# Eight chunks of a modulation product as VectorE dots inside the projections of a later stage

## The reference

```
silu_c = silu(c); silu_cc = silu(c_ctx)
mod_x = silu_c  @ ada_w[layer] + ada_b[layer]
mod_c = silu_cc @ ada_w[layer] + ada_b[layer]
sh1, sc1, g1, sh2, sc2, g2 = split(mod_x, 6)      # the same for mod_c
hx = modulate(rmsnorm(x, norm1_g), sh1, sc1)
x  = x + g1 * (mixer(hx, hc) @ w_out)
x  = x + g2 * squared_relu_mlp(modulate(rmsnorm(x, norm2_g), sh2, sc2))
```

## Time and profile before

| | |
|---|---|
| median of the 3 runs shown | 1949.41 us (1945.05 to 1955.72) |
| span of the profiled execution, first to last instruction | 1942.8 us |
| the profiled execution's own time | not among the times shown; the median lies 6.6 us above the span |
| TensorE busy | 1860.4 us (96%) |
| VectorE, ScalarE, GpSimd busy | 820.1, 585.6, 381.8 us |
| read from HBM | 427.11 MB, mean 220 GB/s |
| mean granted TensorE clock | 0.989 |

### The profile page before, as it was taken

One profiled execution on the slowest core, in us unless ns is written; L12 is line 12 of the kernel. 1 busy time (PEld: TensorE's weight loads), 2 busy tenths in 40 slices (PEclk: granted clock), 3 DMA queues, 4 the chain that ended last, 5 costly groups with the idle time before them and its releaser, 6 DMA issues.

```text
span 1942.8 us, 26199 instructions
## 1 busy us (share of the span) xinstructions
PE 1860.4 (96%) x11266; PEld 1357.8 (70%) x11266; DVE 820.1 (42%) x1345; ACT 585.6 (30%) x892; POOL 381.8 (20%) x201
## 2 busy tenths in 40 slices
PE   6999999999999999999999899999999999889998
PEld 2777796964444344347887757888888788679998
DVE  2625255731111111116342844556665625674333
ACT  2523103231111111113112535222333511544554
POOL 2000000110000000006002031433334150025664
PEclk9999999999999999999999999999999999999999
DMA  9569917679999999992224004345444232414550
GB/s 357 184 239 362 328 44 283 228 305 428 427 427 427 428 427 428 427 401 86 87 87 146 20 33 166 137 174 184 163 152 151 101 117 88 176 51 167 184 196 33
DMA packets 111426, 429.84 MB, mean 221 GB/s; under 512 B 5707, under 2 KB 8822, under 8 KB 98513
## 3 DMA queue, kind: packets, MB, share of 16 engines
q1 hardware_dynamic: 109056, 416.56, 55.3%
q0 software_dynamic: 2256, 11.62, 1.6%
HBM read 427.11 MB, written 1.05 MB: 220 GB/s over the span
## 4 chain that ended last, share of the span: by engine, by line
PE 65%; DMA 17%; DVE 5%; PEld 5%; ACT 3%; issue 3%; POOL 1%; PEldq 0%; SPq 0%; ACTq 0%; POOLq 0%; DVEq 0%
PE bank L572 64%; DMA ring<-in_moe_w_down 7%; PEld bank L572 5%; DMA H<-in_moe_w_down 4%; DMA arena<-in_moe_w_down 4%; DMA X<-in_ctx 1%; PE bank L587 1%; DMA ring<-in_w_in 0%; DVE arena L2541 0%; PEldq L551 0%; DVE ring_low L2617 0%; DVE H L2011 0%; POOL H L1873 0%; DVE ring_low L2193 0%; DVE ring_low L2611 0%
## 5 line engine op out<-in xcount | busy, mean ns | idle before, releaser
L572 PE MATMUL bank<-arena_r,ring_low 128*128 128x512 f32 (+2 forms) x1920 | 594.0, 341 | 1.6 <-DVE H_low L2018 1.0
L572 PE MATMUL bank<-arena_r 128*128 128x256 f32 (+1 forms) x2176 | 589.6, 339 | 5.4 <-POOL arena_r L1966 1.8
L572 PEld LDWEIGHTS bank<-arena_r 128*128 128x128 f32 x2176 | 383.0, 189 | 57.8 <-issue 9.8
L572 PE MATMUL bank<-arena 128*128 128x64 bf16 (+8 forms) x2892 | 362.8, 318 | 41.4 <-DMA arena<-in_hy_filt_w 11.5
L572 PEld LDWEIGHTS bank<-arena_r,ring_low 128*128 128x128 f32 (+1 forms) x1920 | 350.7, 187 | 47.4 <-issue 2.6
L572 PEld LDWEIGHTS bank<-arena 128*128 128x128 bf16 (+4 forms) x2892 | 203.9, 131 | 201.5 <-issue 171.6
L572 PE MATMUL bank<-H_low,arena_r 128*128 128x512 f32 (+1 forms) x672 | 216.3, 339 | 0.0
L572 PE MATMUL bank<-ring,arena 128*64 128x512 f32 x768 | 170.4, 599 | 7.6 <-DMA ring<-in_moe_w_down 7.6
L2599 DVE SCALAR_TENSOR_TENSOR X<-bank,mod,X 128x256 f32<-128x256 f32 x216 | 94.2, 479 | 195.1 <-PE bank L572 195.1
L1950 POOL TENSOR_TENSOR ring_low<-ring,arena_r 128x2048 fp32r<-128x2048 f32 x31 | 142.3, 4613 | 130.0 <-DVE ring_low L2611 68.8
L1426 ACT ACTIVATE arena<-bank 128x512 f32<-128x512 f32 (+2 forms) x106 | 51.1, 496 | 358.5 <-PE bank L572 358.5
(11 more groups left out here) (328 smaller groups left out, 1845.4 us busy)
## 6 DMA issues: line engine op xcount, KB each, us to landing
ring<-in_w_mlp SPq DMA_DIRECT2D x32, 2048.0 KB, 7.8
ring<-in_w_in SPq DMA_DIRECT2D x26, 2048.0 KB, 8.6
ring<-in_ada_w SPq DMA_DIRECT2D x24, 2048.0 KB, 12.2
ring<-in_moe_w_up SPq DMA_DIRECT2D x17, 2048.0 KB, 23.3
ring<-in_moe_w_gate SPq DMA_DIRECT2D x17, 2048.0 KB, 27.8
arena<-in_moe_w_up SPq DMA_DIRECT2D x15, 2048.0 KB, 22.4
ring<-in_moe_w_down SPq DMA_DIRECT2D x14, 2048.0 KB, 23.3
arena<-in_moe_w_down SPq DMA_DIRECT2D x13, 2048.0 KB, 23.7
```

The lines of the kernel that those rows point to most:

```text
L572: ins = nc.tensor.matmul(o, l, r, start=start, stop=stop, skip_group_check=True)
```

## The change

- Modulation chunks 4 to 11 of the second block's first layer are no longer loaded by SP nor multiplied by TensorE. Four chunks stay, all in "hyena" (`GATE_ADA` has four places, the group has four). "projected" has none behind w_in 5, 6 and 7, and `ada_turn(5, ...)`, its copy and its `take_chunk` in "scan_b" go.
- Their 32 blocks of 128 outputs are made on VectorE in l0_in: `block_dots`, two dots of 1024 per block, from `ada_t`, a transposed copy that the host makes. GpSimd brings the blocks, the first 16 in pairs (1 MB) into two places lent by GV and YT, the rest singly (512 KB) into the two halves of the second place; each waits until the place is free. Before it writes GV (j = 5) ScalarE waits for 16 blocks, before YT's second half (j = 6) for all 32.
- In l0_in ScalarE makes the high half of chunks 1 to 6 (`chunk_high`), after the second tile of the chunk before; VectorE only subtracts (`chunk_low`).
- `CSIL` gets a place of its own and is brought and put through Silu early (in "projected" and in expert pair 2) instead of in layer 0's MLP. GpSimd's space for descriptors is set to 8192.

```diff
@@ TensorE and SP, "projected" to "hyena"
-        BEHIND = [[], [0, 1], [2, 3], [4, 5], [6, 7], [8, 9], [10, 11], [12, 13, 14]]
+        BEHIND = [[], [0, 1], [2, 3], [4, 5], [6, 7], [], [], []]
...
-            return WIN + j + sum(len(b) for b in BEHIND[:j]) if j < 8 else WIN + (23, 24, 27, 30)[j - 8]
-
-        GATE_ADA = [WIN + 25, WIN + 26, WIN + 28, WIN + 29, WIN + 31]
+            return WIN + j + sum(len(b) for b in BEHIND[:j]) if j < 8 else WIN + (16, 17, 19, 22)[j - 8]
+
+        GATE_ADA = [WIN + 18, WIN + 20, WIN + 21, WIN + 23]
...
                 load(n, cols(T["w_in"], WIN_ORDER[j] * 512, 512), as_cols(n))
-                for i in BEHIND[j] if j < 8 else ([], [15, 16], [17, 18], [19])[j - 8]:
...
-                    ada_turn(5, 7, 1, 7)
-                    pe.wait_ge(S("ada_out"), 2 + 6)
...
-            ada(GATE_ADA[0], 6, 6, 0, 5)
+            ada(GATE_ADA[0], 5, 6, 0, 4)
...
-            ada(GATE_ADA[1], 6, 6, 1, 5)
             for nt in range(2):
                 gate_tile(10, nt)
...
@@ places
-        ROT = A3(23968, 4, L)
+        ROT, DOT = A3(23968, 4, L), A(23968, D)
...
+        BLOCKS, LENT = 32, 16
+        BLOCK_PAIRS = [A3(o, 2, D) for o in (6144, 10240)]
+
+        def block_slot(q):
+
+            return BLOCK_PAIRS[(q // 2) % 2 if q < LENT else 1][:, q % 2, :]
...
@@ ScalarE
+                if p == 2:
+                    for s in range(2):
+                        act.wait_ge(S(f"blocks_in{s}"), 16)
+                    A_(CSIL, CSIL, ACT.Silu).then_inc(S("silu_c"), 1)
...
+                def chunk_high(j):
+
+                    n = first + 2 * j
+                    act.wait_ge(full[n % RING], arrived(n))
+                    act.wait_ge(used, n + 1 - RING + 1)
+                    A_(low(n + 1), slot(n), ACT.Copy).then_inc(S("high_copied"), 1)
+
+                if l == 0:
+                    chunk_high(1)
                 for j in range(8):
                     for nt in range(1 if j == 7 else 4):
                         o = tile()
+                        if l == 0 and nt == 0 and j in (5, 6):
+                            act.wait_ge(S("dots"), (LENT, BLOCKS)[j - 5])
...
+                        if l == 0 and nt == 1 and 1 <= j < 6:
+                            chunk_high(j + 1)
...
@@ GpSimd
+            def bring_pair(i):
+
+                if i >= 2:
+                    pool.wait_ge(S("dots"), 2 * (i - 1))
+                bring(BLOCK_PAIRS[i % 2], T["ada_t"][2 * i * P:2 * (i + 1) * P, :].rearrange("(b p) d -> p b d", p=P), f"blocks_in{i % 2}")
+
+            def bring_block(q):
+
+                pool.wait_ge(S("dots"), max(LENT, q - 1))
+                bring(block_slot(q), T["ada_t"][q * P:(q + 1) * P, :], f"blocks_in{q % 2}")
...
+                    pool.wait_ge(S("silu_c"), 2)
+                    for i in range(2):
+                        bring_pair(i)
...
                 for h in range(1, 2 + 2 * l):
                     head_args(h)
+                if l == 0:
+                    for i in range(2, LENT // 2):
+                        bring_pair(i)
+                    for q in range(LENT, BLOCKS):
+                        bring_block(q)
...
-                if l == 0:
-                    bring(CSIL, T["c_all_2"].rearrange("p (a d) -> p a d", a=2), "b2_in")
...
@@ VectorE
+                def block_dots(a, n):
+
+                    dve.wait_ge(S("silu_c"), 2)
+                    for q in range(a, a + n):
+                        dve.wait_ge(S(f"blocks_in{(q // 2 if q < LENT else q) % 2}"), block_arrived(q))
+                        for c in range(2):
+                            d = V.scalar_tensor_tensor(DOT, block_slot(q), 1.0, CSIL[:, c, :], ALU.mult, ALU.mult,
+                                                       accum_out=mod[:, 1, 16 + q, c:c + 1])
+                            if c == 0:
+                                link(d)
+                        d.then_inc(S("dots"), 1)
+                        dve.wait_ge(S("dots"), q + 1)
+
+                def chunk_low(j):
+
+                    n = first + 2 * j
+                    dve.wait_ge(S("high_copied"), 10 + j)
+                    V.tensor_tensor(low(n), slot(n), low(n + 1).bitcast(F32), ALU.subtract).then_inc(full[(n + 1) % RING], 16)
+
                 for j in range(1 + l, 5):
-                    split_chunk(first + 2 * j)
+                    if l:
+                        split_chunk(first + 2 * j)
+                        continue
+                    chunk_low(j)
+                    block_dots((0, 5, 11, 17)[j - 1], (5, 6, 6, 5)[j - 1])
...
                 for j in range(5, 7):
-                    split_chunk(first + 2 * j)
+                    if l:
+                        split_chunk(first + 2 * j)
+                        continue
+                    chunk_low(j)
+                    block_dots((22, 28)[j - 5], (6, 4)[j - 5])
...
@@ host
-    nc = _bacc.Bacc("TRN2", target_bir_lowering=False, num_devices=1)
+    nc = _bacc.Bacc("TRN2", target_bir_lowering=False, num_devices=1, dynamic_dma_scratch_size=8192)
```

More of the change, by code:

```diff
@@ L177, in build @@
         et = sb("chunk_decay", [P, 64])
+        CSIL = sb("silu_rows", [P, 2 * D])[:, :].rearrange("p (a d) -> p a d", a=2)
         AR = 25600
@@ L307, in _ @@
                 load(n, cols(T["w_in"], WIN_ORDER[j] * 512, 512), as_cols(n))
-                for i in BEHIND[j] if j < 8 else ([], [15, 16], [17, 18], [19])[j - 8]:
+                for i in BEHIND[j] if j < 8 else ([], [8], [9, 10], [11])[j - 8]:
                     n += 1
@@ L525, in build, with block_arrived @@
         MLP_BANK = (4, 5, 2, 3)
-        CSIL, CPROD = A3(12288, 2, D), A3(22944, 2, D)
+        CPROD = A3(22944, 2, D)
+        BLOCKS, LENT = 32, 16
+        BLOCK_PAIRS = [A3(o, 2, D) for o in (6144, 10240)]
+        def block_slot(q):
+            return BLOCK_PAIRS[(q // 2) % 2 if q < LENT else 1][:, q % 2, :]
+        def block_arrived(q):
+            return 32 + 16 * (q // 4) if q < LENT else 32 + 16 * (LENT // 4 + (q - LENT) // 2)
         W1h_cols, W2h_rows = W1h.rearrange("p (k n) -> p k n", k=KT), W2h.rearrange("p (k n) -> p k n", k=4)
@@ L848, in _ @@
             chunk_used()
-            ada(GATE_ADA[2], 6, 6, 2, 5)
+            ada(GATE_ADA[1], 5, 6, 1, 4)
             pe.wait_ge(S("un_ready"), 2)
             spectrum_half(0)
-            ada(GATE_ADA[3], 6, 6, 3, 5)
+            ada(GATE_ADA[2], 5, 6, 2, 4)
             for nt in range(2):
@@ L858, in _ @@
             chunk_used()
-            ada(GATE_ADA[4], 6, 6, 4, 5)
+            ada(GATE_ADA[3], 5, 6, 3, 4)
             flush()
@@ L865, in _ @@
                        "y_time" if (c, ft) == (3, 3) else None)
-            ada_turn(6, 6, 0, 5)
+            ada_turn(5, 6, 0, 4)
             def merge(nt, side):
@@ L1361, in mlp_pair @@
                             if l == 0 and not early and (nt, ks[-1]) == (3, 3):
-                                pe.wait_ge(S("dots"), 6 * j)
+                                pe.wait_ge(S("dots"), BLOCKS + 6 * j)
                                 chunk_used(2)
                             if (l, j, nt) == (0, 0, 3):
-                                ada_turn(7, 7, 0, 2, ADA_COLS)
+                                ada_turn(6, 7, 0, 2, ADA_COLS)
                         n += 1
@@ L1566, in _ @@
             gate_tiles(14, 2)
-            ada_rows(6, 6, 0)
+            ada_rows(5, 6, 0)
             merge_high(2)
@@ L1666, in _ @@
                 W = 2 * L if l == 0 else L
+                first = (L0, L1)[l]
                 if l:
@@ L1833, in mlp_pair @@
                         if l == 0 and isinstance(i, int) and u == 0:
-                            ada_rows(7, 7, 0, ADA_COLS)
-                            act.wait_ge(S("b2_in"), 16 * 5)
-                            A_(CSIL, CSIL, ACT.Silu).then_inc(S("silu_c"), 1)
+                            ada_rows(6, 7, 0, ADA_COLS)
                 mlp_pair(0)
@@ L1889, in _ @@
             bring(hmask, T["hg_mask"].rearrange("p (a b) -> p a b", a=2), "x_in")
+            for s in range(2):
+                bring(CSIL[:, s, :], T["c_all_2"][:, s * D:(s + 1) * D], f"blocks_in{s}")
             phase_end(pool, "projected")
@@ L2234, in _ @@
             merge_low(3, 0)
-            take_chunk(1, 6, 6, 28, 5)
-            dve.wait_ge(S("ada_out"), 2 + 7)
+            take_chunk(1, 5, 6, 0, 4)
+            dve.wait_ge(S("ada_out"), 2 + 6)
             gains(0, (1,))
-            gains(1)
+            gains(1, (0,))
             V.tensor_tensor(gsc[:, 1, 0, :, 0], gsc[:, 1, 0, :, 0], vec("fin", 0, 8), ALU.mult)
@@ L2435, in _ @@
             for k in range(KT):
-                V.scalar_tensor_tensor(X[:, k, 0:L], X[:, k, 0:L], vec("fin", k), RS1, ALU.mult, ALU.mult)
+                i = V.scalar_tensor_tensor(X[:, k, 0:L], X[:, k, 0:L], vec("fin", k), RS1, ALU.mult, ALU.mult)
+            link(i)
             ncall = 5
@@ L2458, in _ @@
                 for j in range(5, 7):
-                    split_chunk(first + 2 * j)
```

(13 more changed lines are left out.)

23 lines of the change are left out of this document (10 added, 13 removed).

## The result

The changed kernel takes 1954.24 us (median of 8 runs), the kernel before 1948.32 (8 runs on the same occasion): a ratio of 1.0035, 95% interval 1.0019 to 1.0050, some 6 us slower and within the 0.5% that the prediction called "the same". On another occasion it was 1956.32 against 1946.82, ratio 1.0043 (1.0030 to 1.0057). The profiled execution has a span of 1949.5 us against 1942.8. It took 1951.27 us, 1.8 more than its span and the least of its eight; by the same 1.8 the profiled execution of before took some 1944.6 (an estimate), so both profiles show quick ones.

What follows compares the result with a forecast made beforehand. TensorE's matmul line was taken to bound 64.5% of the span, w_down's DMA another 15.7%. A loss of 12 minus a gain of 10.3 gave +1.7 us on 1942.8; with 6.6 from span to median, 1951, range 1941 to 1965.

Steps and rivals of the forecast that it cites:

- The removal in "projected": First block's projections: seven chunks removed gain 7.0 us, not 12.7, as w_in 7 waits for a bank behind `scan_exps(1)`.
- "scan_b": Start of "scan_b": without `ada_turn(5, ...)` and the wait for `mod`, the scores start 1.5 us earlier.
- "hyena": In "hyena" one chunk of five goes from TensorE, a gain of 1.8 us.
- short stalls should cost no clock: TensorE's stalls in l0_in were taken to leave the granted clock unchanged, a cost of 0.
- The loss in l0_in: Second block's first projections: TensorE waits for VectorE's low halves, 3.5 + 8.5 = 12 us.
- Ahead of w_in 5: Window between low halves 4 and 5, with the rotation: VectorE needs 30.5 us against 22.0, TensorE waits 8.5.
- ahead of w_in 6: Window between low halves 5 and 6: VectorE needs 25.5 us against 22.0, TensorE waits 3.5.
- the pairs hold: l0_in, low halves 2 to 4: a pair is fetched (5.6 us) while the other is used (5.0); cost 0.
- Quiet fetches: Rival, chance 0.20: SP's load doesn't hold GpSimd's fetches up in l0_in; loss 5 us, 1944.
- Slow fetches: Rival, chance 0.25: every fetch in l0_in costs what c_all's did; loss 20 to 29 us, 1959 to 1968.
- The dots hide: Rival, chance 0.13: block waits fall where VectorE waits for ScalarE's copy anyway; loss 0.5 us, 1939 or less.
- GpSimd beside the dots: `head_args(1)` in l0_in: each of five instructions may wait 1.15 us for a dot, ending 918 to 924; cost 0.

Runs made afterwards that it cites:

- rotation_out: The changed kernel without the rotation of queries and keys in the first layer; 1946.31 us in a single execution.
- gaps_sized: The changed kernel with 6 and 9 filler matmuls in TensorE's waits ahead of w_in 7 and the second block's w_in 5; 1950.05 us, ratio 1.0002.
- resident_blocks: The changed kernel with only four blocks fetched, once, and all 64 dots reading one of these; 1945.34 us, ratio 0.9980.
- removal_alone: The changed kernel with the eight chunks removed and no blocks or dots in their place; 1941.71 us, ratio 0.9973; again 1940.82, 0.9960.
- removal_gap_filled_2: Second timing of removal_alone with 6 filler matmuls in the wait ahead of w_in 7; 1938.15 us, ratio 0.9947.

## Why the prediction was right, and where it was off

The forecast was 1951, from -10.3 and +12. Against the median of before timed with it (1948.3), the +1.7 gives 1950.0; measured 1954.2. It was right in sign and within its range, 4 us low. The rows place 4 us: 2.2 in "projected" and 1.9 in l0_in, of which 3.8 are low clock. That the two figures agree is partly chance: from span to span the change is +6.7, 5.0 above the forecast, since the stages that the change doesn't touch differ by another 1.1.

**The removal in "projected": 7.0 us predicted, 4.8 measured.** The mechanism held to a tenth: w_in 7 waits for ScalarE's take behind `scan_exps(1)`, 5.93 us against "5 to 6". The full value of the removed work, 12.7, never appeared. The 2.1 us that are missing are the low clock behind the wait. "scan_b" (1.5 predicted, 1.5 measured) and "hyena" (1.8, 2.0) were right.

**The step that failed is "short stalls should cost no clock".** I had read the clock of 0.98 among the experts' waits of 27 us as a sign that short waits cost nothing. It was the mean of a stage in which TensorE is seldom the limit, and says nothing of the matmuls right behind a wait. Measured: the wait of 5.9 us cost 1.5 to 2.1 us (15.60 to 16.18 instead of 14.08), that of 8.6 us 1.7 (24.31 instead of 22.64), that of 2.9 in rotation_out 1.6 (one case), three of 3.9 to 4.2 at the end of the experts 0.9 to 1.5 (16 small matmuls in 2.95 to 3.55 us instead of 2.08), and waits of 0.6 to 1.6 us none (22.22 and 22.23 us behind waits of 1.3 and 0.9, 22.67 in gaps_sized behind 1.60). gaps_sized gives it back. The Trainium skill (TensorE: Matmul & The Clock Gate, "HAM oscillation — how this bites in real kernels") tells of just this, a wait for data after which the next group of matmuls starts at the low clock. The traces agree, and the prediction should have weighed that page.

**The loss in l0_in: 12 predicted, 13.9 measured.** Ahead of w_in 5 8.5 predicted, 8.64 measured; ahead of w_in 6 3.5 and 1.50, where the low clock hid up to 1.7 (rotation_out, without it, has 2.87); ahead of w_in 4 0 and 1.33. The stalls' sum, 11.5 for 12, owes something to luck: 1.33 too little at one place and 2.0 too much at another. The 1.33 comes from the pairs, for which "the pairs hold" gave 0: VectorE waited 5.51 us for one that landed after 10.2, beside a w_in load of 12.5 that began at 929, and 2.48 for one that took 7.2, where 5.6 and 8.7 had been assumed. With the 4.19 for block 16, which the prediction had named, the spare time was gone. 1.7 of low clock and 0.7 for starting three times anew come on top of the stalls, so the term that moved the sum is again the clock, 0 for 1.7. The fetch waits were right, 6 us in each of the last two full windows. VectorE's first dots behind a wait, windows four and five:

```profile
988.17 1.23 DVE L2495 SCALAR_TENSOR_TENSOR arena<-arena,silu_rows 128x1024 f32<-128x1024 f32 x1 [4.54 <-DMA arena<-in_ada_t]
...
994.86 1.23 DVE L2495 SCALAR_TENSOR_TENSOR arena<-arena,silu_rows 128x1024 f32<-128x1024 f32 x1 [1.64 <-DMA arena<-in_ada_t]
...
1019.16 1.23 DVE L2495 SCALAR_TENSOR_TENSOR arena<-arena,silu_rows 128x1024 f32<-128x1024 f32 x1 [4.66 <-DMA arena<-in_ada_t]
...
1025.80 1.22 DVE L2495 SCALAR_TENSOR_TENSOR arena<-arena,silu_rows 128x1024 f32<-128x1024 f32 x1 [1.60 <-DMA arena<-in_ada_t]
```

6.2 and 6.3 us, and made as the prediction had it: 1.7 twice, with 2.9 more for the fetch that meets w_in, would be a wait of 4.6 and one of 1.7. The issues of ada_t show the meeting. Four stretches, 979 to 986, 986 to 999, 1010 to 1016 and 1021 to 1032 us; the number is the median from issue to landing:

```profile
ring<-in_w_in SPq DMA_DIRECT2D x1, 2048.0 KB, 9.2
arena<-in_ada_t POOLq DMA_DIRECT2D x2, 512.0 KB, 6.2
...
arena<-in_ada_t POOLq DMA_DIRECT2D x3, 512.0 KB, 3.8
...
ring<-in_w_in SPq DMA_DIRECT2D x1, 2048.0 KB, 10.9
arena<-in_ada_t POOLq DMA_DIRECT2D x2, 512.0 KB, 6.6
...
arena<-in_ada_t POOLq DMA_DIRECT2D x4, 512.0 KB, 3.8
```

Beside a w_in load the four fetches took 6.7, 5.7, 6.8 and 6.3 us, the other twelve 3.7 to 4.8. I had 3.5 for 512 KB with SP's queue at rest and 6.5 with it busy. The median of all, 3.8, hides the ones that make the long waits. In rotation_out, with the window moved, it is the same: w_in loads at 979 and 1002, fetches of 6.4 us beside them, waits of 4.29 twice. The Trainium skill's figures (DMA: Bandwidth & Descriptors, "Anatomy of one DMA": 2.0 us and 436 GB/s) make an estimate of 3.2, 0.6 under the fetches at rest and far under those beside a load.

**What decided between the rivals.** "Quiet fetches" failed on the four fetches beside w_in: SP's load does hold them up, and each window waited 6.2 us, not 3.4. "Slow fetches" failed on the other twelve, which took about 3.8. "The dots hide" failed because the waits didn't hide; with the fetches gone (resident_blocks) the window of the rotation costs 0.6 us, about what 24.6 us of work against 22 and 2.2 would give.

**GpSimd beside the dots.** `head_args(1)` ended at 915.0, which is 919.8 in the times of before (l0_in begins 4.8 earlier), inside the 918 to 924; the third pair's first dot began at 920.4, or 925.2, inside 924 to 930. Its five instructions took 1.3 to 2.1 us each, 8.2 in all where they took 6.3 before, so a dot beside them cost 0.4 us an instruction and not the 1.15 assumed; the end fell inside the range because the range began with no delay. The dots beside GpSimd took 1.38 to 2.32 instead of 1.22. Timeline of GpSimd:

```profile
897.97 5.39 POOL L1967 TENSOR_TENSOR arena<-arena 128x512 f32<-128x512 f32 x1
...
911.82 1.77 POOL L1969 TENSOR_SCALAR RS<-arena 128x256 f32<-128x256 f32 x1
```

The first stood beside VectorE's subtraction of 4.43 us, as in the earlier trace rows.

**What stays open.** Why TensorE stood still longer at the end of the experts in three kernels. And why "scan_b" ran at a full clock in both halves in three of thirteen profiles and not in the others. It was low with and without the wait ahead of it, and one profile of the kernel before doesn't tell how often it falls there. So far as it falls more often after the change than before, some of the 2.5 us that removal_alone lacks (5.6 and 6.0 us of gain measured, 8.3 by the rows of "projected", "scan_b" and "hyena") is due to that; it wasn't measured.

## What to carry to other kernels

Removed work is worth what is left once the next wait ends, and the wait that then appears on TensorE has a second price, the low clock behind it; price the stall and the tile after it. Such a gap is room that costs nothing: here four chunks kept beside it, with half the dots, made a kernel faster than moving all eight (0.9969 against 1.0035). An engine that fills a window to the last microsecond pays for whatever else lands in it (here a rotation of 7.6 us, and a fetch that took 6.7 us instead of 3.8 because it met the load of the next weight), so put moved work where neither stands. When a load is brought forward, look at which queue is full at that time.

## What the runs showed of the hardware

TensorE's granted clock fell in each of the six profiled executions with a wait of 5.9 us, in none of the seven without it at that place. A filler matmul of 128x512 f32 from a 128x128 identity took 0.87 us a call, in two instructions, nearly four times the 0.23 that I had taken from the matmuls of the second block (96 in 22.2 us). A 512 KB fetch on GpSimd's queue took 3.7 to 4.8 us, and 5.7 to 6.8 beside a 2 MB load of SP's queue. And the low clock in a stage of small matmuls ("scan_b", 32x128 and 128x32) made 1.7 to 8.3 us of difference between profiles (8.3 in removal_gap_filled_2, 32.81 and 31.13 us for the two halves), as much as the whole change.
